# Reordering the opening of a two-layer decoder step, and the orders and PSUM banks of attention's first and last steps

## The reference

```python
for i in range(DEPTH):                      # layer 0: HGRN2, layer 1: attention
    h, gate = adaln(x, c, norm_w[i], ada_w[i], ada_b[i])
    # adaln: ada = silu(c) @ w_ada + b_ada ; shift, scale, gate = split(ada, 3)
    #        h = rmsnorm(x, norm_w) * (1 + scale) + shift
    if i % 2 == 0:
        y, s_new = hgrn2_mixer(h, s0, ...)  # proj = h @ w_in, gated scan, (o*silu(z)) @ w_out
    else:
        y, rows = dilated_mixer(h, ...)     # proj = h @ w_in, rmsnorm+rope of q and k,
                                            # 3 groups of windowed attention, joined by softmax
                                            # of their lse, (o*silu(z)) @ w_out
    x = x + gate * y
```

## Time and profile before

| | |
|---|---|
| median of 3 runs | 1081.74 us (1081.57 to 1081.86) |
| profiled execution's own time | 1079.47 us |
| its span, first to last instruction | 1077.7 us |
| granted clock of PE, mean | 0.999 |
| PE busy | 1059.7 us (98%) |
| DVE busy | 645.2 us (60%) |
| ACT busy | 508.1 us (47%) |
| POOL busy | 149.1 us (14%) |

### The profile page before, as it was taken

The page is one execution under the profiler, slowest core; times in us unless marked ns, Lnnn a source line. Parts: engine busy times, 40 slices in busy tenths (PEclk is TensorE's granted clock), DMA queues, the critical chain, the costliest instruction groups (busy, mean ns, idle before and its releaser), DMA issues.

```text
span 1077.7 us, 24568 instructions
## 1 busy us (share of the span) xinstructions
PE 1059.7 (98%) x10237; PEld 974.4 (90%) x10237; DVE 645.2 (60%) x1301; ACT 508.1 (47%) x1049; POOL 149.1 (14%) x167
## 2 busy tenths in 40 slices
PE   8999999999999999999999999999999999999998
PEld 5799999999999999989998789888988998898997
DVE  4785767676768686875436744644464446347333
ACT  4653444444454545464224455545455464566122
POOL 2000010101000000000000550343035204410000
PEclk9999999999999999999999999999999999999999
DMA  9862536363536364127525454426443544444432
GB/s 322 303 198 85 175 103 179 101 175 105 176 104 177 105 177 143 35 97 246 153 86 164 111 138 127 132 63 160 128 131 91 130 129 117 113 117 111 118 104 59
DMA packets 233300, 147.80 MB, mean 137 GB/s; under 512 B 8899, under 2 KB 227229, under 8 KB 232678
## 3 DMA queue, kind: packets, MB, share of 16 engines
q1 hardware_dynamic: 218544, 134.35, 43.5%
q10 hardware_dynamic: 14646, 11.89, 3.3%
HBM read 124.19 MB, written 22.02 MB: 136 GB/s over the span
## 4 chain that ended last, share of the span: by engine, by line
PE 92%; DVE 3%; ACT 2%; SPq 1%; DMA 1%; issue 1%; POOL 0%; ACTq 0%; DVEq 0%; POOLq 0%
PE PJ L446 27%; PE PJ L1805 17%; PE PJ L1495 16%; PE PJ L467 9%; PE X L1293 2%; PE PJ L1864 1%; PE X L1352 1%; PE X L1954 1%; PE X L1473 1%; PE PJ L754 1%; PE PJ L493 1%; DMA pre<-in_ada_w_dram 1%; PE X L1920 1%; PE X L1475 1%; SPq L2691 1%; PE X L1366 1%
## 5 line engine op out<-in xcount | busy, mean ns | idle before, releaser
L446 PE MATMUL PJ<-h_hi,w_hi 128*128 128x288 f32 (+2 forms) x672 | 147.4, 301 | 0.5 <-ACT v_ L1009 0.5
L446 PE MATMUL PJ<-h_lo,w_hi 128*128 128x288 f32 (+2 forms) x672 | 143.7, 295 | 0.0
L446 PE MATMUL PJ<-h_hi,w_low 128*128 128x288 f32 x672 | 139.9, 296 | 0.0
L446 PEld LDWEIGHTS PJ<-h_hi,w_hi 128*128 128x128 f32 x672 | 108.1, 189 | 3.2 <-issue 3.0
L446 PEld LDWEIGHTS PJ<-h_lo,w_hi 128*128 128x128 f32 x672 | 108.5, 189 | 0.0
L412 ACT ACTIVATE w_hi<-raw 128x1024 fp32r<-128x1024 f32 (+1 forms) x91 | 92.7, 1035 | 32.1 <-PE PJ L1805 16.0
L446 PEld LDWEIGHTS PJ<-h_hi,w_low 128*128 128x128 f32 x672 | 106.5, 189 | 0.0
L467 PE MATMUL PJ<-w_hi,h_hi 128*128 128x256 f32 x320 | 91.1, 292 | 0.8 <-DVE q_ L1129 0.8
L419 DVE TENSOR_TENSOR w_low<-raw,w_hi 128x1024 fp32r<-128x1024 f32 x64 | 77.3, 1224 | 23.8 <-ACT w_hi L412 23.3
L467 PE MATMUL PJ<-w_low,h_hi 128*128 128x256 f32 x320 | 88.0, 283 | 0.0
L1805 PE MATMUL PJ<-w_hi,h_hi 128*128 128x512 f32 x210 | 84.7, 403 | 1.8 <-DVE w_low L419 1.8
(11 more groups left out here) (388 smaller groups left out, 2449.3 us busy)
## 6 DMA issues: line engine op xcount, KB each, us to landing
raw<-in_a_w_in_dram SPq DMA_DIRECT2D x48, 512.0 KB, 4.8
raw<-in_ada_w_dram SPq DMA_DIRECT2D x28, 512.0 KB, 3.8
kvc<-in_cache_kv_w_dram SPq DMA_DIRECT2D x24, 512.0 KB, 5.1
pre<-in_ada_w_dram SPq DMA_DIRECT2D x16, 512.0 KB, 9.9
s<-in_state_hgrn_dram SPq DMA_DIRECT2D x8, 1024.0 KB, 8.3
out_hgrn_sample_dram<-s ACTq DMA_DIRECT2D x8, 1024.0 KB, 5.2
raw<-in_a_w_out_dram SPq DMA_DIRECT2D x16, 512.0 KB, 4.8
raw<-in_b_w_in_dram SPq DMA_DIRECT2D x64, 128.0 KB, 2.3
```

What stands on the lines that cost most here:

```text
L446: last = nc.tensor.matmul(PJ[:, 2 * s + e, 0:n1 - n0], a[:, k, :], b[:, k, n0:n1], start=(k == 0 and i == 0), stop=(k == KD - 1 and i == 2))
```

## The change

In the opening on PE, `first_ada(0)` comes after all eight chunks are turned, the first turn ahead of `first_ada(1)`, `first_ada(2)` ahead of the first chunk, `first_ada(3)` behind chunk 2, and the last turn behind chunk 3. There are 10 unused matmuls in place of 12. Chunks 6 and 7 run ticket by ticket. ACT copies block 2 of FIRST_ADA behind chunk 1. DVE scales chunks 0 and 1 ahead of a copy.

In attention's first step DVE makes the low parts of pieces 4 and 5 ahead of `rope` (0, 2), and those of 6 and 7 ahead of `rope` (0, 3). In the last step `p12` is turned straight behind `p0`, into banks 2 and 3 of `X`; the sequences' probabilities go into banks 0 and 1; `pe_m(j, 2)` writes bank 0, waits for no gate, and comes ahead of `pe_turn`. ACT copies both turned blocks and the sequences' ahead of two sigmoids, and DVE has `seq_weigh` ahead of `scale_p0`.

```diff
@@ first_pe
-                if k == 5:
-                    pe.wait_ge(c_sb, 1)
-                    pe.wait_ge(par_done, 1)
-                    first_ada(0)
+            pe.wait_ge(c_sb, 1)
+            pe.wait_ge(par_done, 1)
+            first_ada(0)
...
             pe.wait_ge(s_fold, 16)
+            turn_ada(adr0[:, 0], 0, ada_t0[:, 0:4])
             pe.wait_ge(x_sb, KD)
             first_ada(1)
-            turn_ada(adr0[:, 0], 0, ada_t0[:, 0:4])
             turn_ada(adr0[:, 2], 1, ada_t0[:, 8:12])
-            for _ in range(12):
+            for _ in range(10):
                 pe.matmul(X[:, 2, 0:P], ones[:], ones[:], start=True, stop=True)
-            for k in range(KD):
-                first_tickets(pe, k)
-                if k == 0:
-                    first_ada(2)
+            first_ada(2)
+            for k in range(KD - 2):
+                first_tickets(pe, k, range(2))
                 if k == 1:
+                    turn_ada(adr0[:, 1], 2, ada_t0[:, 4:8])
+                if k == 2:
                     pe.wait_ge(n_r, 1)
                     first_ada(3)
-                    turn_ada(adr0[:, 1], 2, ada_t0[:, 4:8])
+                if k == 3:
                     turn_ada(adr0[:, 3], 3, ada_t0[:, 12:16])
+            for t in range(2):
+                for k in range(KD - 2, KD):
+                    first_tickets(pe, k, (t,))
@@ first_act
+                if k == 1:
+                    first_ada_rows(act, 2, copy)
                 if k == 3:
-                    first_ada_rows(act, 2, copy)
                     first_ada_rows(act, 3, copy)
@@ first_dve
-            first_ada_rows(dve, 1, dve.tensor_copy)
             scale_x(0)
             scale_x(1)
+            first_ada_rows(dve, 1, dve.tensor_copy)
@@ pe_pt12, pe_pts, pe_m, pe_ms (last_or(a, last, other) is last in step 3)
-            if place(a, PT_ORDER, 1):
-                pe.wait_ge(pt_read, 2 * a + 1)
+            if a == GH - 1:
+                pe.wait_ge(ss_mask, 3 * a + 3)
...
+            else:
+                pe.wait_ge(pt_read, 2 * a + 1)
...
             elif n == 0:
-                pe.wait_ge(ss_mask, 3 * a + 2)
-                pe.wait_ge(pts_read, a + 1)
-            else:
+                pe.wait_ge(pt_read, 2 * a + 2)
+            elif (a, g) != (GH - 1, 2):
                 pe.wait_ge(o_read, 3 * a + n)
@@ pe_last
             pe_pt0(pe, j)
+            pe_pt12(pe, j)
             pe_pts(pe, j, GH)
-            pe_pt12(pe, j)
             pe_m(pe, j, 0)
             pe_ms(pe, j)
             pe_m(pe, j, 1)
+            pe_m(pe, j, 2)
             pe_turn(pe, j)
-            pe_m(pe, j, 2)
@@ act_attention, last step
                 pt_out(j, 0)
+                pt_out(j, 1)
+                pts_out(j)
                 z_sigmoid(10)
-                pts_out(j)
                 z_sigmoid(11)
-                pt_out(j, 1)
@@ dve_attention, first step, then last step
-                rope(0, 2)
                 piece(4)
                 piece(5)
-                rope(0, 3)
+                rope(0, 2)
                 piece(6)
                 piece(7)
+                rope(0, 3)
...
+                seq_weigh(j)
                 scale_p0(j)
-                seq_weigh(j)
```

More of the change, by code:

```diff
@@ L728, in first_pe, with first_tickets @@
             pe.wait_ge(s_fold, 16)
+            turn_ada(adr0[:, 0], 0, ada_t0[:, 0:4])
             pe.wait_ge(x_sb, KD)
             first_ada(1)
-            turn_ada(adr0[:, 0], 0, ada_t0[:, 0:4])
             turn_ada(adr0[:, 2], 1, ada_t0[:, 8:12])
-            for _ in range(12):
+            for _ in range(10):
                 pe.matmul(X[:, 2, 0:P], ones[:], ones[:], start=True, stop=True)
-            for k in range(KD):
-                first_tickets(pe, k)
-                if k == 0:
-                    first_ada(2)
+            first_ada(2)
+            for k in range(KD - 2):
+                first_tickets(pe, k, range(2))
                 if k == 1:
+                    turn_ada(adr0[:, 1], 2, ada_t0[:, 4:8])
+                if k == 2:
                     pe.wait_ge(n_r, 1)
                     first_ada(3)
-                    turn_ada(adr0[:, 1], 2, ada_t0[:, 4:8])
+                if k == 3:
                     turn_ada(adr0[:, 3], 3, ada_t0[:, 12:16])
-        def first_tickets(pe, k):
+            for t in range(2):
+                for k in range(KD - 2, KD):
+                    first_tickets(pe, k, (t,))
+        def first_tickets(pe, k, tickets):
             pe.wait_ge(n_hx, k + 1)
             pe.wait_ge(n_lo, k + 1)
-            for t in range(2):
+            for t in tickets:
                 pe.wait_ge(raw_split, t + 1)
@@ L2025, in pe_pt0, with last_or @@
             last.then_inc(pt_ready, 1)
+        def last_or(a, last, other):
+            return last if a == GH - 1 else other
         def pe_pt12(pe, a):
@@ L2029, in pe_pt12 @@
             pe.wait_ge(kc_read, 4 * a + 4)
-            if place(a, PT_ORDER, 1):
-                pe.wait_ge(pt_read, 2 * a + 1)
+            if a == GH - 1:
+                pe.wait_ge(ss_mask, 3 * a + 3)
             for g in range(2):
                 for r in range(CH):
-                    last = pe.transpose(X[:, g, r * P:(r + 1) * P], p12[:, g, r, :], ident[:])
+                    last = pe.transpose(X[:, last_or(a, 2, 0) + g, r * P:(r + 1) * P], p12[:, g, r, :], ident[:])
             last.then_inc(pt_ready, 1)
@@ L2041, in pe_pts @@
                 pe.wait_ge(a_xn, tile_no(j, 0, 1) + 1)
+            else:
+                pe.wait_ge(pt_read, 2 * a + 1)
             for n in range(4):
-                pe.transpose(X[:, 2, n * P:(n + 1) * P], ps_[:, TILE_AT[n]:TILE_AT[n] + P], ident[:])
+                pe.transpose(X[:, last_or(a, 0, 2), n * P:(n + 1) * P], ps_[:, TILE_AT[n]:TILE_AT[n] + P], ident[:])
             for g in range(3):
@@ L2048, in seq_turned, with o_bank @@
         def seq_turned(a):
-            return (unit_tile(a + 1, 0, 1) if a < GH - 1 else X[:, 3, :])[0:TS, 0:3 * P]
+            return (unit_tile(a + 1, 0, 1) if a < GH - 1 else X[:, 1, :])[0:TS, 0:3 * P]
         def picked(ap, half):
             return ap.rearrange("p (n k i) -> p n k i", k=8, i=16)[:, :, 5 * half:5 * half + 3:2, :]
+        def o_bank(a, g):
+            return X[:, 0 if (a, g) == (GH - 1, 2) else 3, :]
         def pe_m(pe, a, g):
@@ L2073, in pe_m @@
                 for r in range(CH):
-                    last = pe.matmul(X[:, 3, r * P:(r + 1) * P], vr[:, g, r, :], pt[:, g - 1, r * P:(r + 1) * P],
+                    last = pe.matmul(o_bank(a, g)[:, r * P:(r + 1) * P], vr[:, g, r, :], pt[:, g - 1, r * P:(r + 1) * P],
                                      start=True, stop=True)
@@ L2219, in rows_out, with pt_bank @@
                 act.activation(prow.rearrange("p g c -> p (g c)"), X[:, 2, 0:3 * P], ACT.Copy).then_inc(prow_done, 1)
+            def pt_bank(a, i):
+                return last_or(a, 2 * i, 0)
             def pt_out(a, i):
@@ L2225, in pt_out @@
                 act.activation(pt_flat[:, x0:x0 + (2 * TP if i else 7 * P)],
-                               X[:, 0:2, :].rearrange("p e n -> p (e n)")[:, 0:(2 * TP if i else 7 * P)],
+                               X[:, pt_bank(a, i):pt_bank(a, i) + 2, :].rearrange("p e n -> p (e n)")[:, 0:(2 * TP if i else 7 * P)],
                                ACT.Copy).then_inc(pt_read, 1)
@@ L2283, in pts_out @@
                     slots = pz[:].rearrange("p n (x y b) t -> p n x y b t", x=2, y=2)[:, :, :, half, :, 0:DS]
-                    act.activation(slots, picked(X[:, 2, :], half).rearrange("p n x (b t) -> p n x b t", b=2), ACT.Copy)
+                    act.activation(slots, picked(X[:, last_or(a, 0, 2), :], half).rearrange("p n x (b t) -> p n x b t", b=2), ACT.Copy)
                     own_rows = pts[0:TS].rearrange("p n (x y i) -> p n x y i", x=2, y=2)[:, :, :, half]
@@ L2446, in gate_o @@
                 dve.wait_ge(o_ready, 3 * a + place(a, O_ORDER, g) + 1)
-                z, o = oz[:, g * GH + a, 0:TP], X[:, 3, :]
+                z, o = oz[:, g * GH + a, 0:TP], o_bank(a, g)
                 if g == 0:
```

## The result

| | kernel before | changed kernel |
|---|---|---|
| median of 20 runs each, us | 1081.09 (1078.84 to 1081.99) | 1084.51 (1082.57 to 1086.92) |
| span of the profiled execution, us | 1077.7 | 1083.1 |
| mean granted clock of that execution | 0.999 | 0.995 |

The changed kernel is slower. The ratio is 1.0033 (95% interval 1.0026 to 1.0040), so +3.4 to +3.6 us. That is clear of the 0.2% within which I had put 0.63 of the chance. The forecast was 1082.8; the time lies 1.7 us above it, outside the forecast's own range of 1081.0 to 1084.0 and inside that of 8 in 10 (1080.0 to 1084.8). As a difference the miss is larger, +3.4 where +1.1 was forecast: the three runs from which I started had a median 0.65 us above that of the 20.

The account below looks back on a forecast made before the run. PE, busy 98% of the span, was taken as the bound. Opening +2.3, clock +1.2, first step -1.35 and last step -1.05 gave +1.1 on the median 1081.74: 1082.8 us, range 1081.0 to 1084.0 (8 in 10: 1080.0 to 1084.8).

Parts of the forecast that it names:

- The gap: Opening: PE stands still 3.66 us ahead of chunk 4, until 48.5, waiting for other engines' chain behind the last turn.
- The early turn "at 0": Opening: moving the first turn ahead of the second block's matmuls gives nothing, 0 (bounds -0.1 and +0.1).
- The clock falls behind the gap: Opening: the granted clock falls in PE's 3.66 us wait, costing +1.2 us (bounds 0 and 3.3).
- the forecast ticket: Opening: PE's ticket that waits for DVE's q_ starts at 55.3, not 53.02, so the opening costs +2.3 us.
- First step, -1.35: Attention's first step: PE's 1.75 us wait for a low part goes, about 0.4 comes back: -1.35 us.
- the 0.4 us that tile 4 was to take back: Attention's first step: PE asks for the next rb at 626.5, it comes at 627.0, returning about 0.4 us.
- Last step, -1.05: Attention's last step: the output projection starts at 989.75, not 990.81: -1.05 us (bounds -1.3 and 0).
- The sum: Whole kernel: opening +2.3, clock +1.2, first step -1.35, last step -1.05, together +1.1 us.
- Within 0.2%: Whole kernel: the measured time differs from no change by at most about 0.2%, or 2.2 us; chance 0.63.
- POOL rival: Attention's first step: POOL becomes the bound and the 1.35 gain is lost, +2.45 or 1084.2 us; chance 0.19.

Follow-up runs that it names:

- e1: The kernel before with only the opening's three functions from the changed kernel, attention as before: 1085.63 us, ratio 1.0039 to the kernel before.
- e4: The changed kernel with 14 more unused matmuls in the gap ahead of chunk 4: 1081.07 us, ratio 0.9998 to the kernel before.
- e5: The changed kernel with the first turn back behind the second block's matmuls: 1083.95 us, ratio 1.0018 to the kernel before.
- e6: The changed kernel with the last block's matmuls and both late turns back behind chunk 1: 1078.86 us, ratio 0.9977 to the kernel before.
- e9: The changed kernel with 12 in place of 10 unused matmuls in the opening: 1081.66 us, ratio 1.0002 to the kernel before.
- e7: The kernel before with only DVE's changed order in attention's first step: 1079.92 us, ratio 0.9985 to the kernel before.
- e11: e6 with 12 in place of 10 unused matmuls in the opening: 1077.31 us, ratio 0.9968 to the kernel before.
- e12: The kernel before with 14 in place of 12 unused matmuls in the opening: 1082.76 us, ratio 1.0017 to the kernel before.

## Why the prediction was right or wrong

- **The gap.** Right. I forecast PE's stop at 44.8 to 48.5; it came at 45.30 to 48.95, with 3.66 us to the hundredth. In `e1`, `e4` and `e5`, where the clock held up to the gap, chunk 4 starts at 48.00 to 48.11, against 48.5 forecast. `e6` shows that the place of the last turn makes the gap. The profile puts it down to "issue" and not to DVE's h_lo as forecast.
- **The early turn "at 0".** Right in place, wrong about what may hang on it. The turn waits 1.35 us for DVE's copy, which the second block's matmuls covered before and which I had not seen. With the clock full this costs nothing: first_ada(2) starts at 32.15 in `e1` and 32.21 in `e4`, as forecast (32.3), because its DMA is what it waits for. In the changed kernel's profile the clock fell at 30.1 us, first_ada(2) started at 32.72 behind slower unused matmuls and ran for the most part at half clock, and the last turn ended 0.5 us later than forecast. I had no term for a fall there.
- **The clock falls behind the gap.** Right, at +1.2 forecast. Measured it is 1.3 (`e1`, `e9`) to 2.6 (`e5`), and 2.1 in the changed kernel's profile, so my term was near the lower end. I had priced it by the 1.5 us that the kernel's first 24 records cost, and deducted 0.3 for DVE's fills. In the changed kernel it lasted for 5 us of work, and DVE's q_ was no longer what PE waited for: PE had no idle time ahead of the ticket at 57.83. With the clock held the forecast ticket was 55.3, and `e4` has 54.87, so the rest of that sum stands. Opening and this clock together: forecast +3.5; measured +3.12 in `e1`, +4.46 in `e5` and +4.81 in the changed kernel. The spread of the changed kernel's runs goes with the clock too: its five shortest spans (1080.8 to 1081.6) have a mean clock of 0.997 or 0.998, its three longest (1084.3 to 1085.1) 0.993 to 0.995.
- **First step, -1.35.** Right: -1.33, and -1.4 alone in `e7`. The parts differ. The low part took 1.94 us, longer than the 1.63 I allowed, so 0.63 us of wait stayed and the start came 1.10 us earlier, not 1.7. But the 0.4 us that tile 4 was to take back were not taken, POOL did not become the bound, and the unit's first matmuls ran 0.23 us faster than before.
- **Last step, -1.05.** Right: -0.95 in both. The gate is what PE waits for, as forecast.
- **The sum.** +1.1 forecast. By the profiles +2.5 (4.81 - 1.33 - 0.95), and layer 0 on top, +2.85, which no step of mine had. In that profile the sum is thus off by 1.3 for the opening with its clock and by 2.85 for layer 0.
- **From profile to median.** I added the difference to the median of 1081.74 although the profiled execution was 2.27 us below it, and didn't ask what those 2.27 us were. I take it that the kernel before pays the waits of layer 0 in most of its runs and the changed kernel in nearly all, so that starting from the median put much of this cost into the forecast by luck. From the profiled execution I had forecast 1080.6, and the changed kernel's took 1084.85. All of this is inferred: none of the longer runs of before was profiled. It fits that the medians differ by 3.4 us and the profiles by 5.4, a difference of 2.0.
- **Chances.** "Within 0.2%" needed the opening's cost not to exceed the gains by 2.2 us. The measured time is near the 1084.2 of the POOL rival, which did not come true. What carried it there is the clock, which fell for longer than I had priced and, in the profile, in one more place; the waits in layer 0 did the rest.

## What to carry to other kernels

When work is moved ahead of a chain's producer, ask what PE can still run while the chain runs. Here two chunks held back covered 3.3 us of such a chain; without them the gap was 3.66 us, and 1.3 to 2.6 us of half clock came on top. Read such a price from more than one profile: the same opening lost 3.12 us in one and 4.81 in another. When a profiled execution lies at the low end of its kernel's runs, find what it lacks before adding a forecast to the median. For differences of 0.2%, look at the shift of the same instruction through the whole trace, since untouched code may answer too.

## What the runs showed of the hardware

- In 9 of the 14 profiles PE stood still in layer 0 for 0.70 to 2.04 us without a releaser, at one or both of two records 256 apart, each time 2.2 to 2.9 us behind the start of a 16 KB transfer of the instruction queue. That PE had run out of instructions fits this; it is inferred.
- Two unused matmuls more, 440 us earlier, went with the absence of these waits in `e9` and `e11` and not in `e12`.
- Behind each idle time of 3.66 us (the changed kernel, `e1`, `e5`, `e9`) the granted clock was at its lower level for 3.4 to 6.1 us of PE's work, which cost 1.3 to 2.6 us. With PE kept at work in that time (`e4`) it stayed full.
- Behind shorter waits it fell in some executions and not in others: with 1.35 us in the changed kernel, 1.29 in `e11`, 0.61 in `e9` and 2.04 in layer 0 of `e12`, not with 1.60 us in `e5` nor 1.75 in attention. So the single wait ahead doesn't tell it.
